# PEER encoder on one core: dense V blocks loaded in pairs, two slots of 1 MB for four of 512 KB

## What is computed

```python
def peer_ffn(xn, w_query, sub_keys, u, v):       # u, v: (128 * 128 experts, 2048)
    q = (xn @ w_query).reshape(b, s, 8, 2, 128)
    sc = einsum('bshpc,hpnc->bshpn', q, sub_keys)
    s_top, i_top = lax.top_k(sc, 16)              # of 128 first keys, of 128 second keys
    cand = s_top[..., 0, :, None] + s_top[..., 1, None, :]
    cand_idx = i_top[..., 0, :, None] * 128 + i_top[..., 1, None, :]
    best, pos = lax.top_k(cand, 16)
    expert = take_along_axis(cand_idx, pos)       # 8 heads x 16 experts for each token
    gate = softmax(best)
    act = gelu(einsum('tkd,td->tk', u[expert], xt))
    return einsum('tk,tkd->td', gate * act, v[expert])
```

## Time and profile before

| | us |
|---|---|
| median of 3 runs | 3062.55 (3060.83 to 3067.06) |
| profiled execution, its own time | 3057.64 |
| its span, first to last instruction | 3055.8 |
| V stage, layer 0, dense blocks begin | 1285 |
| V stage, layer 1, dense blocks begin | 2572 |

### The profile page before, as it was taken

One profiled execution on the slowest core, in us unless ns is written; L12 is line 12 of the kernel. 1 busy time (PEld: TensorE's weight loads), 2 busy tenths in 40 slices (PEclk: granted clock), 3 DMA queues, 4 the chain that ended last, 5 costly groups with the idle time before them and its releaser, 6 DMA issues.

```text
span 3055.8 us, 26007 instructions
## 1 busy us (share of the span) xinstructions
PE 2271.4 (74%) x9280; PEld 1691.7 (55%) x9280; DVE 2173.0 (71%) x3241; ACT 678.1 (22%) x1647; POOL 1010.2 (33%) x1028
## 2 busy tenths in 40 slices
PE   8999999688853300999999587888444019999994
PEld 4685545577853300666666356778333007666662
DVE  1342122899999999856666748999999988566667
ACT  1242120112229920300000021212399002000000
POOL 0000000433343333344444514333433334445444
PEclk9999999899985555999999888999755559999997
DMA  5333324899999999699999959999999996999998
GB/s 211 143 125 140 116 110 198 358 421 420 403 380 422 421 422 418 208 410 409 409 409 409 372 215 423 416 421 393 392 421 422 422 412 216 410 409 409 409 409 331
DMA packets 194528, 1059.08 MB, mean 347 GB/s; under 512 B 21856, under 2 KB 22240, under 8 KB 121312
## 3 DMA queue, kind: packets, MB, share of 16 engines
q0 software_dynamic: 147456, 805.37, 65.3%
q1 hardware_dynamic: 46944, 252.06, 20.8%
HBM read 1055.24 MB, written 2.10 MB: 346 GB/s over the span
## 4 chain that ended last, share of the span: by engine, by line
DMA 46%; PE 25%; DVE 24%; issue 3%; POOL 1%; ACT 1%; DVEq 0%; SPq 0%; ACTq 0%; POOLq 0%
DMA xnT<-pvg,idx_all 23%; DMA arena<-pu,idx_all 20%; DVE arena L1141 11%; PE bank L1299 6%; DVE h L1167 4%; PE bank L1384 3%; PE bank L1539 2%; DMA arena<-pvg,idx_all 2%; PE bank L1605 2%; PE bank L1613 2%; PE bank L1573 2%; PE low L1504 1%; PE low L1493 1%; PE bank L1493 1%; PE bank L1580 1%
## 5 line engine op out<-in xcount | busy, mean ns | idle before, releaser
L1141 DVE CUSTOM_DVE_ANT_0 arena<-arena,low 128x2048 f32<-128x2048 f32 x420 | 951.9, 2286 | 74.2 <-DMA arena<-pu,idx_all 73.0
L449 POOL DMA_INDIRECT arena<-pu,idx_all x456 | 458.8, 1006 | 1367.0 <-DVE cst L1141 702.8
L1622 PE MATMUL low<-arena 128*128 128x512 f32 x2048 | 879.3, 592 | 0.0
L1622 PEld LDWEIGHTS low<-arena 128*128 128x128 f32 x2048 | 604.7, 295 | 274.4 <-issue 0.5
L1167 DVE SCALAR_TENSOR_TENSOR h<-arena,cst,h 128x1024 f32<-128x1024 f32 x240 | 308.1, 1286 | 161.7 <-DMA arena<-pvg,idx_all 160.0
L1167 DVE SCALAR_TENSOR_TENSOR h<-xnT,cst,h 128x1024 f32<-128x1024 f32 x240 | 307.6, 1286 | 161.3 <-DMA xnT<-pvg,idx_all 159.7
L464 POOL DMA_INDIRECT arena<-pvg,idx_all x256 | 248.9, 972 | 296.0 <-DVE h L1167 216.3
L464 POOL DMA_INDIRECT xnT<-pvg,idx_all x256 | 246.9, 965 | 290.7 <-DVE h L1167 222.5
L1605 PE MATMUL bank<-arena 128*128 128x128 f32 x512 | 132.9, 441 | 201.4 <-ACT arena L734 201.4
L497 ACT ACTIVATE arena<-h 128x2048 f32<-128x2048 f32 x10 | 19.1, 1907 | 1041.2 <-DVE h L1199 945.7
L1573 PE MATMUL bank<-xnT,arena 128*128 128x128 f32 x1792 | 242.8, 286 | 0.0
(11 more groups left out here) (229 smaller groups left out, 2203.9 us busy)
## 6 DMA issues: line engine op xcount, KB each, us to landing
arena<-pvd SPq DMA_DIRECT2D x256, 512.0 KB, 6.8
arena<-w_proj SPq DMA_DIRECT2D x22, 2048.0 KB, 7.7
arena<-wq SPq DMA_DIRECT2D x16, 2048.0 KB, 11.9
arena<-w_out SPq DMA_DIRECT2D x9, 2048.0 KB, 7.6
arena<-pu,idx_all POOLq DMA_INDIRECT x494, 14.8
gB<-gains SPq DMA_DIRECT2D x5, 1024.0 KB, 10.0
xnT<-pvg,idx_all POOLq DMA_INDIRECT x256, 14.6
arena<-pvg,idx_all POOLq DMA_INDIRECT x256, 14.6
```

The costliest lines, as they stand in the source:

```text
L449: nc.gpsimd.indirect_dma_start(U[t][slot], None, pu[L], bass.IndirectOffsetOnAxis(row(n), 0)).then_inc(u_got[t][slot], 16)
L1141: vec.tensor_tensor_reduce(out=u, in0=u, in1=low[:, :] if staged else xns[t], scale=1.0, scalar=0.0, op0=ALU.mult, op1=ALU.add, accum_out= ...
L1622: ins = mm(psum[2 * t + c][:, 0:VH], W[t][:, :, n], vdense[:, n % DR, c * VH:(c + 1) * VH], start=n == 0, stop=n == NK - 1)
```

## The change

Blocks of two successive second keys are stored next to each other, so that a partition's row is 8 KB, and are loaded together: 64 loads of 1 MB a layer through DR = 2 slots, in place of 128 loads of 512 KB through four. The space is the same. `dense` waits at even n for the pair's load, and raises `vd_used` at odd n, when the pair is read. The gains load stands behind load 8 in place of load 16, which are the same keys. The matmuls and their order stay.

```diff
--- before.py
+++ after.py
@@ -55,7 +55,7 @@
 UT0, UT1, UP = 6, 7, 3
 VD, VG = 1024, D - 1024
 VH = VD // 2
-VR, DR = 8, 4
+VR, DR = 8, 2
 POOLW = (2, 4, 8, 16)
 HK = PH * PK
 BANDS = (((0, P + max(POOLW) // 2),), ((P - max(POOLW) // 2, P + max(POOLW) // 2), (P + max(POOLW) // 2, S)))
@@ -174,7 +174,7 @@
         xnT_flat = xnT[:, :, :].rearrange("p k s -> p (k s)")
         vslots = [xnT_flat[:, i * VG:(i + 1) * VG] for i in range(4)]
         vslots += [arena[:, V_AT + i * VG:V_AT + (i + 1) * VG] for i in range(VR - 4)]
-        vdense = carver(VD_AT, W_AT)(DR, VD)
+        vdense = carver(VD_AT, W_AT)(DR, 2, VD)
         goh1 = gB[:, 0:2 * QT * P].rearrange("p (b i n) -> p b i n", b=2, i=QT)
         goh2 = gB[:, 2 * QT * P:4 * QT * P].rearrange("p (b i n) -> p b i n", b=2, i=QT)
 
@@ -372,19 +372,19 @@
             def load_vd(L, n):
 
                 if n >= DR:
-                    sp.wait_ge(s["vd_used"], L * (NK - 1) + n - DR + 1)
+                    sp.wait_ge(s["vd_used"], L * (NK // 2 - 1) + n - DR + 1)
                 else:
                     sp.wait_ge(s["dot_done"], (L + 1) * NDOT)
-                sp.dma_start(vdense[:, n % DR], pvd[L][n]).then_inc(vd_got[n % DR], 16)
+                sp.dma_start(vdense[:, n % DR].rearrange("p b c -> p (b c)"), pvd[L][n]).then_inc(vd_got[n % DR], 16)
 
             for L in range(LAYERS):
                 for hd in range(2, PH):
 
                     sp.wait_ge(s["q_mm"], EVENTS * L + hd + 1)
                     load_wq(L, hd)
-                for n in range(NK):
+                for n in range(NK // 2):
                     load_vd(L, n)
-                    if n == 16:
+                    if n == 8:
 
                         sp.wait_ge(s["spread_mm"], TB * QUADS * (L + 1))
                         gain(2 + 2 * L)
@@ -1616,12 +1616,15 @@
 
             def dense(L, n):
 
-                pe.wait_ge(vd_got[n % DR], L * 16 * NK // DR + landed(n, DR))
+                b = n % 2
+                if b == 0:
+                    pe.wait_ge(vd_got[n // 2 % DR], L * 16 * NK // 2 // DR + landed(n // 2, DR))
                 for t in range(TB):
                     for c in range(2):
-                        ins = mm(psum[2 * t + c][:, 0:VH], W[t][:, :, n], vdense[:, n % DR, c * VH:(c + 1) * VH],
+                        ins = mm(psum[2 * t + c][:, 0:VH], W[t][:, :, n], vdense[:, n // 2 % DR, b, c * VH:(c + 1) * VH],
                                  start=n == 0, stop=n == NK - 1)
-                ins.then_inc(s["dense_done" if n == NK - 1 else "vd_used"], 1)
+                if b:
+                    ins.then_inc(s["dense_done" if n == NK - 1 else "vd_used"], 1)
 
             for L in range(LAYERS):
                 if L:
@@ -1726,7 +1729,7 @@
 
     def by_second_key(v):
 
-        return v.reshape(NK, NK, D)[:, :, :VD].transpose(1, 0, 2)
+        return v.reshape(NK, NK // 2, 2, D)[:, :, :, :VD].transpose(1, 0, 2, 3).reshape(NK // 2, NK, -1)
 
     w_in = a["w_in"][0]
     aq, ak, av = AH * AD, AH * AD + AKV * AD, AH * AD + 2 * AKV * AD
```

## The result

The changed kernel takes 3112.29 us (median of four runs, 3109.97 to 3114.52), the kernel before 3061.69 (four runs). The ratio is 1.0167, with a 95% interval of 1.0153 to 1.0182: slower by some 51 us. The forecast was 3105, with a range of 3071 to 3134. The profiled execution of the changed kernel took 3109.97 us, its span 3108.2.

What follows compares the result with a forecast made beforehand. V-row gathers were taken to set the V stage's end, dense finishing 31 us before needed. Late pair loads would add 22 us a layer: 3057.64 + 44 = 3102, with most of 4.9 on top 3105 us; range 3071 to 3134.

Steps and rivals of the forecast that it cites:

- Sign, place and mechanism: Slower, chance 0.86: in both layers' V stages TensorE waits for late pair loads, so dense ends after the gathers.
- the pairs were not in time: Rival for the dense loads: pairs arrive in time, only 4.6 us a layer gained, 3053 us; chance 0.10.
- the rows were not cut: Rival for the dense loads: DMA cuts rows to 4 KB, 8.4 us a pair, 3156 us; chance 0.02.
- the clock did not stay at half: Rival for the dense matmuls: stalls take TensorE to 1.2 GHz, 13.7 us a pair, 3880 us; chance 0.02.
- The landing of 1 MB: Dense V load beside the gathers, issue to landing: 4.25 + 3.8 = 8.05 us, bounds 4.8 and 10.1.
- 4.25 us: Part of a dense load's landing independent of size: start behind the gathers and completion, 6.8 - 2.55.
- The stall: TensorE in the dense stage: 8.68 us needed, 6.87 covered, standing 1.8 us every second pair; 7.78 us a pair.
- the step of the stage: V stage end: dense sums added at 1777.6 in place of 1755.65, 22 us later per layer, 44 in both.
- the 3102 of the sum: Whole kernel, profiled execution: 3057.64 + 44 = 3102 us.
- The undisturbed turn: Dense matmuls beside the gathers: two pairs take 6.87 + 8.68 = 15.55 us.
- The rows of 8 KB: Dense V loads: 422 GB/s against 410, 4.6 us less per layer while the gathers set the end.
- The matmuls after layer 0's stage: First matmuls after the stage, slow after a 38.5 us pause: 1 or 2 us could come back, not counted.

Runs made afterwards that it cites:

- pairs_filled_two: Changed kernel plus two unread extra matmuls ahead of TensorE's wait for each pair from the third to the 57th: 3106.97 us, ratio 1.0166.
- pairs_filled: Changed kernel plus four unread extra matmuls ahead of TensorE's wait for each pair from the third on: 3143.47 us, ratio 1.0262.
- pairs_no_gathers: Changed kernel without the 240 gathers of V rows per layer and their adds: 3000.51 us (one run).
- singles_three_slots: The kernel before with three slots of 512 KB in place of four: 3060.65 us, ratio 0.9998.
- pairs_two_loads: Changed kernel with each slot filled by two 512 KB loads in 4 KB rows, both waited for: 3187.69 us, ratio 1.0412.
- singles_two_slots: The kernel before with two slots of 512 KB in place of four: 3390.64 us (one run).

## Why the prediction was right

**Sign, place and mechanism** came out as forecast, and the rivals fell: the pairs were not in time, the rows were not cut (q1 moves 53.93 MB in 7400 packets), and the clock did not stay at half.

**The landing of 1 MB**, the term on which all hung, was 8.0 us for 8.05. It could be had from the trace of the kernel before, by differences between loads that stood directly behind one another. The two rows of 1 MB as they stood, 4.8 and 10.1 us, would have given a gain of 9 us or a loss of over 120. What the 4.25 us in it are made of (the start behind the gathers, the completion) is not shown.

**The stall**: 7.87 us a pair measured, 7.78 forecast. The adds went at 1.89 us for 1.90 and ended at 1736.4 for 1737. The dense sums were added at 1782.4 for 1777.6.

**What was undersized** is the step of the stage: 26.6 and 27.6 us a layer measured, 22 worked out. The profiled execution lay 8 us above the 3102 of the sum. The trace takes the difference apart. The stretch from pair 2's first matmul to pair 57's lies beside the gathers. It is 55 pairs and took 433.0 us in layer 0 (1300.91 to 1733.96) and 434.9 in layer 1; at 7.78 a pair it would be 428. Three terms differ, and they partly cancel.

*The undisturbed turn was taken too long.* Where no landing is late and the clock is full, two pairs take 15.25 us (median), not 15.55: the landing is 7.95, and what stands around it 7.3 in place of 7.5. The first matmul begins 0.04 us after the landing, so the 0.43 us for loading weights does not stand there. This gives 419 us, 8 less than the forecast's 428.

*Every eighth load lands late*, in about 9.3 us (8.8 to 9.7), and its pair starts some 1.3 us later. TensorE's timeline shows one in the third line, and below it is that load, issued at 1363.2:

```profile
1355.95 7.24 PE L1624 MATMUL low<-arena 128*128 128x512 f32 x16 [0.35 <-DMA arena<-pvd]
1363.67 7.24 PE L1624 MATMUL low<-arena 128*128 128x512 f32 x16 [0.48 <-DMA arena<-pvd]
1372.48 14.11 PE L1624 MATMUL low<-arena 128*128 128x512 f32 x32 [1.57 <-DMA arena<-pvd]
...
arena<-pvd SPq DMA_DIRECT2D x1, 1024.0 KB, 9.2
```

While each of these loads is under way, seven a layer, the trace has one packet of 16 KB on queue q8, of kind "instruction", that takes 0.9 to 1.1 us; a single other load of the two stretches takes over 8.7. The queue's packets in 1300 to 1700 us, of the changed kernel, of pairs_filled_two and of pairs_filled, rise with TensorE's instructions (16, 20 and 24 matmul records a pair):

```profile
q8 instruction: 7, 0.11, 0.1%
...
q8 instruction: 8, 0.13, 0.1%
...
q8 instruction: 9, 0.15, 0.2%
```

In pairs_filled they come 5.3 pairs apart, and the landings over 9 us with them. In pairs_no_gathers the same packets delay nothing (4.8 us with and without). So I read them as TensorE's instructions being fetched, on DMA engines that are full; no run takes them away.

*The clock.* The forecast had it at 1.00 through the stage, with a rival at half throughout; short stretches after single pauses it did not have. A pair with such a stretch in it takes 8.94 us in place of 7.24.

Both reach the end nearly whole. Eight undisturbed pairs are 61.0 us; with one late landing eight take 62.2 to 63.0, with a half-clock stretch too 63.6 to 64.2. That is some 10 us a layer for the landings, and 5 and 6 for the clock. With the 419 they come to 434 and 435 us, against 433.0 and 434.9. It also says why pairs_filled_two gave back only 1.7 and 3.9 us: with the clock held it saves 5 and 6, and its extra matmuls bring nine and eight such packets in this stretch in place of seven.

So the mechanism and the landing were right, and the nearness of the number was partly luck: terms of some 15 us a layer were missing, and a turn taken too long hid about half of them.

**The small terms.** The rows of 8 KB, with loads of 1 MB, were worth 4 us a stage for 4.6, in the kernel with three slots, where the gathers still set the end. The matmuls after layer 0's stage came back by 0.9 us (forecast 1 to 2, not counted):

```profile
1790.01 3.73 PE L1639 MATMUL low<-arena 128*128 128x136 f32 x16 [7.61 <-DVE arena L820]
1793.57 2.02 PE L1639 MATMUL bank<-arena 128*128 128x136 f32 x16
```

3.73 + 2.02 us against 3.96 + 2.71, after a pause of 7.6 us instead of 38.5.

The Trainium skill's advice of 1 MB or more per DMA (DMA: Bandwidth & Descriptors, "Rules for kernel authors") holds in the run where the landing was covered: loads of 1 MB in rows of 8 KB took 4 us off each stage. Its fit of the time per DMA, given under "Anatomy of one DMA" for the path that GpSimd issues on, makes 1 MB an estimate of 4.4 us. These loads are SP's; it comes near their 4.8 us in the kernel without gathers, and not near the 8.0 us beside them.

## What to carry to other kernels

The same bytes in half as many slots of double size are not the same cover. What covers a load is the work on the slots in between, (slots - 1) x work per slot, 10.3 us with four and 6.87 with two here, while the larger load also lands later, so compare need and landing under the traffic of that very stage. Here that landing could be had from loads that queue directly behind one another. An engine's waits are free as long as its stage partner ends later (in singles_three_slots the dense matmuls took 27 and 29 us longer and the time did not move), and dear from there on. Look at the late landings too, not at the median alone. If the large load is wanted, free or wait in halves, or find a third slot; that was the faster kernel here.

## What was not expected of the hardware

In the changed kernel TensorE paused for 2.4 us at most and was still some 90% busy overall (366 of 400 us), and yet there were short stretches at half clock, 1.2 GHz, three in one stage and four in the other. Each of the seven followed a pause of 1.8 to 2.4 us; after six other pauses of the same lengths the clock stayed at 2.4 GHz. The U stage's row with the same busy share at full clock did not warn of it. With longer pauses (up to 3.6 and 4.3 us) there was more of it: granted clock 0.94 in pairs_two_loads, 0.80 in singles_two_slots.

A pvd load of 1 MB landed in 8.0 us with up to eight gathers outstanding, in 7.9 with four, in 6.9 with two and in 4.8 with none (medians). Beside eight, the loads that ran together with a 16 KB instruction packet took about 9.3 us.
